# Attention loop: the copies of the turned probabilities and the second half's sinks, moved among the steps

## The reference, cut to what matters

```python
# q: 16 heads of 64, k and v: 2 heads of 64; 16 chunks of 64 tokens; keys: own chunk and the one before
scores = einsum('bnqhgd,bnkhd->bnhgqk', q, kk) * HEAD_DIM ** -0.5     # masked in chunk 0's missing keys
m = maximum(max(scores, axis=-1), sink)
p = exp(scores - m)
probs = p / (sum(p, axis=-1) + exp(sink - m))
o = einsum('bnhgqk,bnkhd->bnqhgd', probs, vv)                        # then o @ w_o
```

## Time and profile before

| | us |
|---|---|
| median of 3 runs (lowest, highest) | 2333.36 (2329.72, 2334.00) |
| the profiled execution: its own time | 2332.27 |
| its span | 2330.4 |
| TensorE busy in the span (matmuls) | 2275.2 (98%) |
| VectorE busy | 1309.0 (56%) |
| ScalarE busy | 710.1 (30%) |
| GpSimd busy | 802.8 (34%) |
| TensorE's mean granted clock | 0.992 of full speed |

### The profile page before, as it was taken

How to read it: one execution, slowest core, us unless ns; L and a number is a source line. 1 busy time by engine, 2 the same in 40 slices (tenths; PEclk the granted TensorE clock), 3 DMA queues, 4 the chain that set the end, 5 groups by cost and what they waited for, 6 DMA issues and landing times.

```text
span 2330.4 us, 29117 instructions
## 1 busy us (share of the span) xinstructions
PE 2275.2 (98%) x10252; PEld 1816.7 (78%) x10252; DVE 1309.0 (56%) x1643; ACT 710.1 (30%) x975; POOL 802.8 (34%) x622
## 2 busy tenths in 40 slices
PE   6998999999999999999999999999999999999998
PEld 4785687888888888777888888877788888888886
DVE  8688788566566564564334521456654555555555
ACT  4327443223223222233222211223323223322322
POOL 0223412553554452301211122121154445355354
PEclk8999999999999999999999999999999999999999
DMA  6462522222212213223333221222111111111112
GB/s 256 127 176 71 212 94 73 73 64 81 90 53 82 85 51 107 90 91 110 119 132 127 88 72 45 82 72 90 55 46 46 54 54 45 45 63 36 54 55 91
DMA packets 84299, 201.38 MB, mean 86 GB/s; under 512 B 23937, under 2 KB 29953, under 8 KB 83714
## 3 DMA queue, kind: packets, MB, share of 16 engines
q1 hardware_dynamic: 65826, 139.70, 18.9%
q10 hardware_dynamic: 18400, 60.69, 7.5%
HBM read 182.54 MB, written 16.78 MB: 86 GB/s over the span
## 4 chain that ended last, share of the span: by engine, by line
PE 87%; issue 10%; DVE 1%; ACT 1%; POOL 1%; DMA 0%; DVEq 0%; POOLq 0%; ACTq 0%
PE pp L1560 59%; PE pp L1868 24%; PE pp L1949 1%; POOL w_lo L426 1%; PE pp L1923 1%; PE pp L1776 1%; ACT pr L681 1%; PE pp L1787 1%; PE pp L1750 0%; PE pp L1656 0%; PE pp L1677 0%; DVE small L1293 0%; DVE mod_t L1005 0%; ACT h_hi L694 0%; DVE h_lo L1040 0%
## 5 line engine op out<-in xcount | busy, mean ns | idle before, releaser
L426 POOL TENSOR_TENSOR w_lo<-w_raw,w_hi 128x1024 fp32r<-128x1024 f32 x136 | 329.3, 2422 | 1191.5 <-ACT w_hi L512 1191.5
L1560 PE MATMUL pp<-h_hi,w_hi 128*128 128x512 f32 x1824 | 602.6, 400 | 16.5 <-DVE h_lo L1154 7.0
L1560 PE MATMUL pp<-h_lo,w_hi 128*128 128x512 f32 x1824 | 594.8, 396 | 0.0
L1560 PE MATMUL pp<-h_hi,w_lo 128*128 128x512 f32 x1824 | 594.5, 396 | 0.0
L1413 DVE SCALAR_TENSOR_TENSOR x<-pp,mod,x 128x512 f32<-128x512 f32 x392 | 294.4, 751 | 282.5 <-PE pp L1868 282.5
L1560 PEld LDWEIGHTS pp<-h_hi,w_hi 128*128 128x128 f32 x1824 | 339.5, 188 | 104.2 <-DVE h_lo L1040 11.4
L1560 PEld LDWEIGHTS pp<-h_hi,w_lo 128*128 128x128 f32 x1824 | 343.4, 188 | 83.2
L1560 PEld LDWEIGHTS pp<-h_lo,w_hi 128*128 128x128 f32 x1824 | 343.6, 188 | 81.7
L512 ACT ACTIVATE w_hi<-w_raw 128x1024 fp32r<-128x1024 f32 x162 | 171.3, 1057 | 593.1 <-PE pp L1560 467.9
L1868 PE MATMUL pp<-c_hi,w_hi 128*128 128x512 f32 x784 | 311.4, 397 | 3.1 <-DVE x L1413 3.1
L1868 PE MATMUL pp<-c_lo,w_hi 128*128 128x512 f32 x784 | 311.2, 397 | 0.0
(11 more groups left out here) (183 smaller groups left out, 2234.9 us busy)
## 6 DMA issues: line engine op xcount, KB each, us to landing
w_raw<-weights SPq DMA_DIRECT2D x218, 512.0 KB, 3.6
mod_t<-mod_w ACTq DMA_DIRECT2D x64, 512.0 KB, 4.1
mod_first<-mod_w SPq DMA_DIRECT2D x16, 512.0 KB, 15.3
mod_late<-mod_w ACTq DMA_DIRECT2D x2, 4096.0 KB, 22.3
v_dram<-v_out ACTq DMA_DIRECT2D x16, 512.0 KB, 5.2
vf<-v_dram ACTq DMA_DIRECT2D x16, 512.0 KB, 3.3
x<-x_in SPq DMA_DIRECT2D x4, 1024.0 KB, 8.0
qf<-q_dram SPq DMA_DIRECT2D x32, 128.0 KB, 2.2
```

Of the source, the lines that this page charges most:

```text
L426: nc.gpsimd.tensor_tensor(out=w_lo[:, s, :, :], in0=w_raw[:, s, :, :], in1=w_hi[:, s, :, :].bitcast(f32), op=ALU.subtract).then_inc(lo_don ...
L1560: last = T.matmul((pp[s] if tile is None else tile)[:, cs], w[:, s, k, :], r[:, k, cs], start=(k == 0 and w is w_hi and r is hi), stop=(k ...
```

## The change

ScalarE copies step t-3 in its step t in place of step t-2, still behind the exponentials. VectorE copies step t-3 in place of t-2 too, and its copy moves from behind the sums to ahead of them, behind the maxima. The sinks of steps 16 and 17 are written one step of the loop earlier and behind that step's maxima. TensorE's, GpSimd's and SyncE's programs are the same.

```diff
--- before.py
+++ after.py
@@ -699,8 +699,8 @@
                 if t < 2:
                     values(2 * t)
                     values(2 * t + 1)
-                if 2 <= t < STEPS + 2 and not copied_by_vector(t - 2):
-                    probs_copy(t - 2)
+                if 3 <= t < STEPS + 3 and not copied_by_vector(t - 3):
+                    probs_copy(t - 3)
                 if t % 2 == 0 and t >= 4:
                     out_high(t // 2 - 2)
                 if t == STEPS - 1:
@@ -1306,17 +1306,17 @@
                                 op=ALU.subtract).then_inc(o_lo, 1)
 
             for t in range(STEPS + 4):
-                if t in (NCH, NCH + 1):
-                    dve.wait_ge(p_exp, t - 1)
-                    sinks(t, 1)
                 if t < STEPS:
                     maxima(t)
+                if t in (NCH - 1, NCH):
+                    dve.wait_ge(p_exp, t)
+                    sinks(t + 1, 1)
+                if 3 <= t < STEPS + 3 and copied_by_vector(t - 3):
+                    probs_copy(t - 3)
                 if t == 1:
                     normed(3)
                 if 1 <= t < STEPS + 1:
                     sums(t - 1)
-                if 2 <= t < STEPS + 2 and copied_by_vector(t - 2):
-                    probs_copy(t - 2)
                 if t % 2 and t >= 5:
                     out_low((t - 1) // 2 - 2)
```

## The result

The change makes the kernel slower: 2339.80 us median of 7 runs (2336.87 to 2342.93) against 2332.16 for 7 runs of the kernel before (2328.44 to 2334.00), a ratio of 1.0036 with a 95% interval of 1.0026 to 1.0046. That is 7.6 us by the medians.

What follows compares the result with a forecast made beforehand. The prediction took the attention loop's cross-engine chain of waits, where TensorE waits, as the bound; +9.4 (steps), -2.3 (sinks) and +0.1 (tail) gave +7.2 us, so 2340 us, range 2336 to 2344, widened to 2334 to 2345.

Steps and rivals of the forecast that it cites:

- The period: Attention loop: longest path through the engines' waits over four steps takes 10.41 us against 8.72, +0.42 per step.
- the sinks: Scores 15 to 17 in the loop: 4.9 us for 7.23, so -2.3 us, clock loss included.
- Rival C: Attention loop: nothing replaces the removed waits, VectorE bounds the period at 7.43 us; 2321 us, chance 0.05.
- Rival B: Attention loop: shortest loop through the moved copy decides, 8.6 us for four steps, no change; 2329 us, chance 0.08.
- Rival D: Scores 16 and 17 wait for something else, so the earlier sinks bring nothing; 2341.8 us, chance 0.08.
- the tail: Past scores 31, TensorE fills its waits with output projection products: +0.1 us, bounds 0 and 1.
- the stretches outside the sinks: The 23 steps between scores 6 and 31 not about the sinks: +9.4 us, walked one by one.
- the full clock for the loop: TensorE stays at 2.4 GHz throughout the loop, 70% busy, with no single wait over 1.9 us.
- Rival A: Attention loop: longer waits bring TensorE to half clock for the whole loop, period 13.0 us; 2354 us, chance 0.06.

Runs made afterwards that it cites:

- the fastest kernel: Changed kernel with all copies on ScalarE at step t-2, turn ahead of mix, out_high and out_low one step later: 2319.75 us against 2329.84 for the kernel before.

## Why the prediction was right

The predicted 2340 was met (2339.80). That the totals agree within 0.2 us is luck in part: the measured difference of 7.6 us has an interval of 6.1 to 10.7, and two executions of the change lay 3.1 us apart behind the loop. What bears the forecast out is the loop itself, +7.2 us forecast and +7.3 in the first profile, step by step:

- *The period.* Forecast 10.41 against 8.72, measured 10.48. Each term was a duration between the same two kinds of instructions in the loop of before, and each came out within 0.03 us of it; only their order changed.
- *ScalarE's copies are the cost.* Put in one after the other, by the medians: the sinks -3.1 us; VectorE's copy added to them (ScalarE's put back) -5.5, so 2.4 more; ScalarE's copies on top +7.6, so +13.1 for them. By the last scores the same three are -1.0, -3.8 and +12.0. The parts depend on the order: on the sinks alone, without VectorE's move, ScalarE's copies cost 21.7 us (18.6 + 3.1), a part of it at half clock. The forecast had named both mechanisms, the mix behind the exponentials and out_high's wait of 0.75 us, and the trace has both. How the cost divides between them is known only roughly: with the outputs later the period fell from 10.48 to 9.49, and 9.49 is 1.35 over the 8.14 of ScalarE's copies put back, but out_low moved along with out_high.
- *Rival C* fell as it was set up: out_high did wait, 0.75 us. *Rival B* needed VectorE's maxima early, and the exponentials waited 1.66 us for them. *Rival D* fell: scores 15 to 17 took 4.88 us, 4.9 forecast.
- *The steps and the tail.* The last scores at 256.54, forecast 256.5: the stretches outside the sinks gave +9.5 (forecast +9.4), the sinks -2.35 (-2.3), the tail 0.1 (0.1).
- *The clock, in part wrong.* The forecast kept the full clock for the loop because no wait was to be as long as the 2.94 us of before. The first profile bears this out, but the reason given does not hold: with the sinks alone the clock fell behind a wait of 1.55 us; with VectorE's copies put back it was down for much of the loop; and in the second profile of the change it fell near the end. Rival A is not another case but a share of some runs. In the change the clock cost nothing in one profile and some 2.2 us in the other. The forecast of a full clock held in the first profile, not for the reason given.

The Trainium skill's page "TensorE: Matmul & The Clock Gate" (section "HAM oscillation — how this bites in real kernels"), which the forecast weighed, describes a kernel that falls back to the throttled clock behind each of its waits for a DMA, of about 3 to 5 us. No wait of TensorE in this loop was that long, so that description does not by itself give rival A for waits of 1.9 us, as the forecast had it. The traces here show falls behind waits of 1.55 to 1.86 us all the same, and show that they do not come behind each such wait.

## What to carry to other kernels

Taking a wait away from an instruction by issuing it later can move the wait to whoever reads its result, as with ScalarE's copies here; VectorE's, issued later too, gained. Count what now stands ahead of the instruction in its queue, and look for an instruction just behind it that waits for its reader. In loops spread over in-order queues, walk one period through all waits with durations from the trace, and look at the longest closed path instead of the engine's busy shares: it gave this loop's period at full clock within 1% for five new orders. The order that paid most puts the producer (turn) ahead of independent work (mix), so that its reader works meanwhile; it was not tried without the other moves of that run.

## What the runs showed of the hardware that was not expected

The granted clock of TensorE can fall to 1.2 GHz behind single waits of 1.5 to 1.9 us: 1.55 us for a sink (the sinks alone, 214.66) and 1.86 us for a DMA (ScalarE's copies put back, 191.55). It need not: with the sinks alone, a wait of 1.78 us for the same DMA passed at full clock, 1.00 from 190 to 194 us,

```profile
191.86 0.71 PE L1750 MATMUL pp<-kf,qf 64*128 64x128 f32 x8 [1.78 <-DMA qf<-q_dram]
```

and so did one of 2.7 us in the fastest kernel. A wait of 1.77 us in every period of the change passed at 2.4 GHz for the whole loop in one execution and not in another. What decides this was not settled. It goes with orders that wait much being both slower and more spread: with VectorE's copies put back 18.6 us were lost where the walk at full clock gave 11.5, and the timed runs lay 7.7 us apart, for 1.9 us with ScalarE's copies put back.
